# Adding up the seven products of a Strassen-like up projection in PSUM banks instead of on VectorE

## What is computed

```python
def rms_norm(x, g):
    xf = x.astype(jnp.float32)
    y = xf * lax.rsqrt(jnp.mean(xf * xf, axis=-1, keepdims=True) + EPS)
    return (y * g.astype(jnp.float32)).astype(x.dtype)

def sq_relu_mlp(h, w_up, w_down):
    return jnp.square(jax.nn.relu(h @ w_up)) @ w_down

# in each of the two layers
h = h + sq_relu_mlp(rms_norm(h, g_mlp[layer]), w_mlp_up[layer], w_mlp_down[layer])
```

## Time and profile before

| | us |
|---|---|
| median of 3 runs | 1628.29 |
| the runs | 1630.63, 1628.01, 1628.29 |
| the profiled execution | 1630.15 |
| its span | 1628.40 |

### The profile page before, as it was taken

One profiled execution on the slowest core, in us unless ns is written; L12 is line 12 of the kernel. 1 busy time (PEld: TensorE's weight loads), 2 busy tenths in 40 slices (PEclk: granted clock), 3 DMA queues, 4 the chain that ended last, 5 costly groups with the idle time before them and its releaser, 6 DMA issues.

```text
span 1628.4 us, 29172 instructions
## 1 busy us (share of the span) xinstructions
PE 1598.7 (98%) x12203; PEld 1417.2 (87%) x12203; DVE 1016.4 (62%) x1416; ACT 725.8 (45%) x1144; POOL 271.0 (17%) x222
## 2 busy tenths in 40 slices
PE   8999999999999999999999999999999999989998
PEld 7998677899999999999887898888887788667896
DVE  6534666388666666555557867677756547856544
ACT  5533554465444444331235544444445445675323
POOL 1002212132222222110004222222212000000200
PEclk9999999999999999999999999999999999999999
DMA  6231030123332222232232333222256676001001
GB/s 197 78 78 31 22 84 10 54 78 130 104 104 89 94 84 99 84 99 93 88 104 78 130 104 104 96 90 100 97 103 99 118 96 89 19 1 62 28 28 52
DMA packets 122689, 134.29 MB, mean 82 GB/s; under 512 B 18877, under 2 KB 99508, under 8 KB 122564
## 3 DMA queue, kind: packets, MB, share of 16 engines
q1 hardware_dynamic: 122362, 132.44, 29.7%
q10 hardware_dynamic: 202, 0.06, 0.0%
HBM read 126.13 MB, written 2.10 MB: 79 GB/s over the span
## 4 chain that ended last, share of the span: by engine, by line
PE 91%; DVE 4%; ACT 2%; issue 1%; DMA 1%; SPq 1%; ACTq 0%; DVEq 0%
PE ps L483 30%; PE ps L1703 22%; PE ps L1650 17%; PE ps L2699 2%; PE ps L829 2%; PE ps L1674 2%; PE ps L812 2%; PE ps L939 1%; PE ps L1220 1%; PE ps L2427 1%; PE ps L837 1%; PE ps L3224 1%; PE ps L2871 1%; PE ps L2850 1%; PE ps L2866 1%
## 5 line engine op out<-in xcount | busy, mean ns | idle before, releaser
L453 ACT ACTIVATE w_hi<-raw 128x1024 fp32r<-128x1024 f32 (+2 forms) x171 | 179.4, 1051 | 400.4 <-PE ps L483 249.4
L483 PE MATMUL ps<-x_hi,w_hi 128*128 128x512 f32 (+4 forms) x872 | 245.8, 333 | 0.5 <-DVE x_lo L503 0.4
L483 PE MATMUL ps<-x_lo,w_hi 128*128 128x512 f32 (+4 forms) x872 | 239.7, 326 | 0.0
L483 PE MATMUL ps<-x_hi,w_lo 128*128 128x512 f32 (+4 forms) x872 | 239.1, 325 | 0.0
L460 DVE TENSOR_TENSOR w_lo<-raw,w_hi 128x1024 fp32r<-128x1024 f32 (+2 forms) x171 | 206.5, 1222 | 45.1 <-ACT w_hi L453 45.1
L1703 PE MATMUL ps<-a_hi,w_hi 128*128 128x258 f32 (+1 forms) x768 | 204.2, 320 | 0.3 <-DVE h L1887 0.3
L1703 PE MATMUL ps<-a_hi,w_lo 128*128 128x258 f32 (+1 forms) x768 | 204.1, 320 | 0.0
L1703 PE MATMUL ps<-a_lo,w_hi 128*128 128x258 f32 (+1 forms) x768 | 204.0, 320 | 0.0
L483 PEld LDWEIGHTS ps<-x_hi,w_hi 128*128 128x128 f32 (+2 forms) x872 | 145.4, 187 | 19.2 <-issue 3.1
L483 PEld LDWEIGHTS ps<-x_lo,w_hi 128*128 128x128 f32 (+2 forms) x872 | 144.6, 186 | 16.4 <-issue 2.2
L483 PEld LDWEIGHTS ps<-x_hi,w_lo 128*128 128x128 f32 (+2 forms) x872 | 144.6, 187 | 14.7
(11 more groups left out here) (489 smaller groups left out, 3343.2 us busy)
## 6 DMA issues: line engine op xcount, KB each, us to landing
raw<-in_w_mlp_up SPq DMA_DIRECT2D x32, 1024.0 KB, 5.3
raw<-in_w_mlp_down SPq DMA_DIRECT2D x32, 1024.0 KB, 5.0
raw<-in_w_in SPq DMA_DIRECT2D x16, 1024.0 KB, 9.6
raw<-in_w_in_conv SPq DMA_DIRECT2D x12, 1024.0 KB, 5.0
raw<-in_w_in_attn SPq DMA_DIRECT2D x8, 1024.0 KB, 5.2
raw<-in_w_out_attn SPq DMA_DIRECT2D x4, 1024.0 KB, 5.0
raw<-in_w_out_conv SPq DMA_DIRECT2D x4, 1024.0 KB, 4.9
raw<-in_w_out SPq DMA_DIRECT2D x4, 1024.0 KB, 5.8
```

Of the source, the lines that this page charges most:

```text
L453: act.activation(split_tile(w_hi, t), raw_tile(t), ACT.Copy).then_inc(w_hi_ok, 1)
L483: ins = pe.matmul(tile_banks(t)[0:m, b, 0:c], w[:, k, :], x[:, k, x0:x0 + c], start=(k == order[0] and n == 0), stop=(k == order[-1] and n ...
```

## The change

The products run in the order 1, 7, 6, 2, 5, 4, 3. Bank 0 takes products 1, 6, 5 and 3 in turn, each accumulated on what is there. After product 1 ScalarE copies bank 0 into bank 1, in PSUM, and product 2 accumulates on that copy; the other two copies (bank 2 after product 7, bank 0 after product 6) go to SBUF as before. So the quarters "11" (bank 1) and "12" (bank 0) are finished in PSUM, and VectorE takes each out with one instruction that also does the maximum with zero and the scale. "22" and "21" stay one addition each, with one full-width scaling behind them. The sum "75" and the scaling of tile 0 are gone, bank 3 is no longer used by the products. TensorE waits for ScalarE's first copy ahead of product 6 (now third), for its third copy ahead of product 5 (now fifth) and for VectorE's "22" ahead of product 3 (now last). Tile 1 is squared and split before tile 0.

```diff
-        ORDER = (1, 5, 7, 2, 6, 3, 4)
+        ORDER = (1, 7, 6, 2, 5, 4, 3)
-        P_BANK = {1: 0, 6: 0, 2: 1, 7: 2, 4: 2, 5: 3, 3: 3}
+        P_BANK = {1: 0, 6: 0, 5: 0, 3: 0, 2: 1, 7: 2, 4: 2}
...
             if m == 1:
                 pe.wait_ge(w_lo_ok, t + 1)
-                if first:
-                    pe.wait_ge(evicted, MLP_T0[layer] + 2)
-                else:
-                    pe.wait_ge(copied, 3 * n)
-            if m == 5:
+                pe.wait_ge(evicted, MLP_T0[layer] + 2 if first else up_tile(layer, u - 1) + 2)
+            if m == 7:
                 pe.wait_ge(p_lo, 2 * n + 1)
                 if first:
                     pe.wait_ge(xs["lo"], 4 * layer + 4)
                 else:
-                    pe.wait_ge(added, 3 * n)
-            if m == 7 and not first:
-                pe.wait_ge(evicted, up_tile(layer, u - 1) + 2)
-            if m == 2 and not first:
-                pe.wait_ge(evicted, up_tile(layer, u - 1) + 1)
+                    pe.wait_ge(added, 2 * n)
             if m == 6:
                 pe.wait_ge(copied, 3 * n + 1)
                 pe.wait_ge(p_lo, 2 * n + 2)
-            if m == 3:
-                pe.wait_ge(added, 3 * n + 1)
+            if m == 5:
+                pe.wait_ge(copied, 3 * n + 3)
             if m == 4:
                 pe.wait_ge(w_lo_ok, t + 2)
                 pe.wait_ge(copied, 3 * n + 2)
+            if m == 3:
+                pe.wait_ge(added, 2 * n + 1)
...
-                    if m == 4 and k == 0 and j < 2:
+                    if m == 3 and k == 0 and j < 2:
                         ins.then_inc(mm_done, 1)
...
-            m, dst = ((1, s1), (7, s7), (6, s6))[which]
+            m, dst = ((1, ps[:, P_BANK[2], :]), (7, s7), (6, s6))[which]
             act.wait_ge(product, product_at(layer, u, m))
...
+            elif which == 0:
+                act.wait_ge(evicted, MLP_T0[layer] + 2)
             act.activation(dst[:, 0:hw], ps[:, P_BANK[m], 0:hw], ACT.Copy).then_inc(copied, 1)
...
             if what == "11":
                 dve.wait_ge(product, product_at(layer, u, 2))
-                dve.wait_ge(copied, 3 * n + 1)
-                dve.wait_ge(a_lo_ok, FF // P * layer + 2 * u - 1)
-                dve.tensor_tensor(tmp[:, 0, hw:2 * hw], s1[:, 0:hw], b1, ALU.add).then_inc(evicted, 1)
+                dve.wait_ge(a_lo_ok, read)
+                dve.scalar_tensor_tensor(tmp[:, 0, hw:2 * hw], b1, 0.0, scale_bc[:, f + hw:f + 2 * hw], ALU.max, ALU.mult).then_inc(evicted, 1)
...
+            if what == "22":
+                dve.wait_ge(copied, 3 * n + 2)
+                dve.wait_ge(product, product_at(layer, u, 5))
+                dve.tensor_tensor(tmp[:, 1, 0:hw], s7[:, 0:hw], b0, ALU.add).then_inc(added, 1)
...
             if what == "12":
                 dve.wait_ge(product, product_at(layer, u, 3))
-                dve.tensor_tensor(tmp[:, 0, 0:hw], s6[:, 0:hw], b3, ALU.add).then_inc(added, 1)
...
+                dve.scalar_tensor_tensor(tmp[:, 0, 0:hw], b0, 0.0, scale_bc[:, f:f + hw], ALU.max, ALU.mult).then_inc(evicted, 1)
...
-                add("75")
                 add("11")
                 add("22")
+                add("21")
+                scale_dve(dve, nm, layer, u)
                 add("12")
-                scale_dve(dve, nm, layer, u, 0)
-                add("21")
-                scale_dve(dve, nm, layer, u, 1)
...
             if u <= NU:
+                a_low(dve, nm, layer, u - 1, 1)
                 a_low(dve, nm, layer, u - 1, 0)
-                a_low(dve, nm, layer, u - 1, 1)
```

## The result

The changed kernel took 1640.52 us (median of 5 executions, 1636.55 to 1643.23), the kernel before 1629.76 us beside it (5 executions, 1628.01 to 1630.63). The ratio is 1.0069, with a 95% interval of 1.0051 to 1.0086. It is slower, as foretold, but by 10.8 us where 4.6 were forecast, and 1640.5 lies above the range of 1629.3 to 1636.6. The profiled execution took 1640.52 us, with a span of 1638.7; that of before had 1628.4. Between the two spans lie 10.3 us.

The account below looks back on a forecast made before the run. TensorE, busy 98% of the span, was taken as the bound. Two waits less one removed, 2.52 + 2.67 - 0.58 = +4.61 us on a median of 1628.29, gave 1632.9 us, range 1629.3 to 1636.6.

Parts of the forecast that it names:

- rival A: The clock falls in the two stalls of the layers' first up blocks, 1.7 us each: +8.0, 1636.3 us; chance 0.12.
- The waits: First up block of each layer: position 3 waits for ScalarE's late first copy, 2.52 us in layer 0, 2.67 in layer 1.
- The wait of L1698: Down block behind layer 1's first up block: its wait goes, -0.58 us, or about 0.1 won if low parts stay slow.
- The copy into PSUM: ScalarE's first copy taken as 0.39 us, bounds 0.21 and 0.78; shifts the two stalls by -0.36 to +0.78 us together.
- Settled blocks and VectorE's load: The 26 settled up blocks cost nothing, with 0.73 to 0.80 us of room; 36 us less on VectorE gains nothing.
- C: Less VectorE and ScalarE traffic speeds up the up blocks' matmuls; at 0.3 us per block -3.8, 1624.5 us; chance 0.04.
- D: Settled up blocks wait too; with a first copy of 1.3 us +9.8, 1638.1 us; chance 0.05.
- B: One of the two first-up-block stalls is not paid: +2.1 or +2.5, 1630.6 us, no net change; chance 0.17.
- the statement about later stages: Behind the changed blocks, a wait elsewhere follows TensorE's own work and moves along with the delay; no cost was added.

Follow-up runs that it names:

- e2: Changed kernel with 18 matmuls into free bank 3 ahead of the waiting product 6 in each layer's first up block; 1639.39 us, ratio 1.0059.
- e8: Changed kernel with ScalarE's first copy moved ahead of the weight splits in layer 0 only; 1634.56 us, ratio 1.0026.
- e3: Changed kernel with ScalarE's first copy moved ahead of the last plain square and both weight splits in each layer's first up block; 1628.61 us, ratio 0.9994.
- e9: Kernel before with 66 matmuls (7.9 us) added at the start of layer 0's first up block; 1637.31 us, ratio 1.0052.
- e4: Changed kernel with the first copy ahead of the splits and the second weight split behind the copies, in each layer's first up block; 1628.81 us, ratio 0.9996.
- e1: Kernel before with only a wait for ScalarE's first copy added at position 3 in each layer's first up block; 1636.45 us, ratio 1.0040.
- e5: Changed kernel, unaltered and measured anew; 1640.99 us, ratio 1.0067.
- e10: e4 with 66 matmuls added at the start of layer 0's first up block; 1639.02 us, ratio 1.0056.
- e11: e4 with 43 matmuls (5.1 us) added at the start of layer 0's first up block; 1636.59 us, ratio 1.0042.
- e12: Changed kernel with 8 matmuls (0.95 us) added in layer 1 at the start of the block behind the waiting one; 1637.65 us, ratio 1.0048.
- e15: Changed kernel with 28 matmuls (3.3 us) added in layer 1 at the start of the block behind the waiting one; 1643.55 us, ratio 1.0074.

## Why the prediction was right in part and wrong in size

The sum of the waits held. Two things were missing from it: the falls of the clock behind the waits, which the prediction had only as its rival A, and the late stretch, which it didn't have at all.

**The waits: right, place and size.** Layer 0: the waiting matmul would have started at 372.63 + 0.12 = 372.75 and started at 375.12, 2.37 late; the next start came 0.22 behind it where 0.12 is the rhythm, 0.10 of refill. That makes 2.47, and 2.52 was forecast. Layer 1: 911.33 less 2.44 of idle time and 0.28 of the last record puts that matmul's start at 908.61, so the natural start at 908.73; 2.60 and 0.10 make 2.70, forecast 2.67. As stages, without falls, the first measured 2.62 (e2) and the second 2.47 and 2.35 (e2, e8).

**The wait of L1698: right, and eaten up by small things.** In the down block behind the first up block of layer 1 the low parts ran free of GpSimd, as said, in 0.69 us each where before two of them took 3.52:

```profile
921.57 0.69 DVE L1820 TENSOR_TENSOR a_lo<-tmp,a_hi 128x512 fp32r<-128x512 f32 x1 [0.88 <-ACT a_hi L1735]
```

The wait is gone from the page. But of the 0.58 us only 0.2 to 0.35 stand in stage B (2.70 against 2.47 and 2.35), and e3, which has no such wait either, has a stage B of 650.77 against 650.72 of before. The price itself was right: in e9, the kernel before with nothing but a delay, the wait is gone as well and stage B is 650.15, 0.57 us shorter. In the new order it is used up in layer 1 by a first up block of 10.12 us against 9.96 (e3), by twelve settled up blocks that alternate between 9.97 and 9.94 us where before it was 9.95 and 9.94 (119.46 against 119.34 us in all), and by twelve down blocks of 11.14 us against 11.11 (133.68 against 133.35). Why these take longer was not looked into; the prediction had put them at nothing.

**The copy into PSUM: in its bounds.** Durations of the copies by destination (ns: least, median, most):

```profile
L1721 ACT ACTIVATE s<-ps x56: 364/387/389, 375.0 to 1188.8; 128x258 f32<-128x258 f32 x28, 128x256 f32<-128x256 f32 x28
L1721 ACT ACTIVATE ps<-ps x28: 362/368/370, 374.7 to 1186.0; 128x258 f32<-128x258 f32 x14, 128x256 f32<-128x256 f32 x14
```

0.37 us was measured where 0.39 was taken from the earlier trace rows. The Trainium skill (ScalarE: Activation LUTs, Step-by-step: what each stage is for), which says that ScalarE reaches PSUM faster, agrees with this trace, by 0.02 us.

**Settled blocks and VectorE's load: right.** The other 26 up blocks wait for nothing. A stretch of the chain in layer 0:

```profile
384.07 11.54 PE ps L1698 x96
...
438.88 10.05 PE ps L1645 x84
```

That is the 10.05 of the earlier trace rows; its down blocks take 11.54 to 11.61 us, around the 11.60 there. Rivals C (less traffic makes matmuls faster) and D (settled blocks wait) are refuted by these, C also by e3 and e4. B (a wait is swallowed) is refuted by the two waits of the changed kernel, which stages A and B both show at full price, and by e1.

**The clock: the first step that failed.** The prediction named the mechanism as rival A, priced it, and gave it 0.12, with the sentence that "the matmuls around these stalls are dense, those before the fall weren't". That reason was worth nothing: in 12 of 15 such waits the clock fell although the matmuls on both sides were dense. The price was right within 0.3 us: 1.53 and 1.44 measured by stages, 1.7 forecast. That waits and falls together came to 8.0 us in e5's stages, as rival A had said, is in part luck: its falls were 0.4 us too dear and its waits, less the 0.58, 0.5 us too cheap. The Trainium skill (TensorE: Matmul & The Clock Gate, Why this matters for your kernels) warns of idle gaps between bursts of matmuls only where they are longer than these. Here the clock fell at gaps of 2.2 to 2.5 us in 12 of 15 cases, so by the measurement shorter gaps count too. The step should have weighed as what they are, 1.3 us of idle time in 4 (4.00 - 2.73) followed by a fall, with waits of nearly twice that to come.

**The late stretch: what no step held.** The sum ended at the stages of the change, and the statement about later stages was that a delay moves along. The late part moves along, but it doesn't cost the same in every execution: 104.3 to 105.0 us undisturbed, 108.9 to 109.0 with 10.2 us at half clock, 110.0 to 110.2 with 13.7. A term of about 4.7 us for it was put at nothing. The kernel before has the late stretch seldom, if at all (none is profiled with it): its executions are mostly from 1627.8 to 1630.5, and four of the 23 beside e1 lie from 1632.3 to 1634.2. The changed kernel has it in nine of eleven, by the same measure.

**The sum as measured**, for the profiled executions: waits 2.62 + 2.47, falls 1.53 + 1.44, stage D 4.19 (late stretch 4.7, missing fall at 1508 us -0.5), the missing fall at 269 us -1.94, the untouched stages -0.01; together 10.3 us. The forecast had the first two terms, less 0.58, and nothing else. It also started from a median of before of 1628.29, which five executions put at 1629.76, so that against the forecast of 1632.9 the result is 7.6 us off and the difference 6.2.

**What stays open.** Why the late stretch comes in nine of eleven executions of the changed kernel and, by their times, in all of e2's, in one to three of six with a pure delay of 5 to 8 us, and in none of 22 of e3 and e4, isn't settled. That it needs the long waits or the falls behind them is excluded (e2 has no such fall, e10 neither, and both have it), and so is that they always bring it (e5 has both and is without it). Whether they make it more frequent isn't. That a shift of the late part alone can bring it is shown by e10 and e11 against e3 and e4 (5 of 12 executions by their times, two of them with a profile, against none of 22); that single microseconds decide is suggested by the steps of e12 to e15 within the spread of six executions. Which moment is a bad one can't be told from these traces, since executions of one kernel differ.

## What to carry to other kernels

When a change gives a wait less room, look at the first pass through the loop apart from the settled ones: there the releasing engine still comes from other work, and here all of the loss started from two places out of 28, while one instruction moved ahead of that work took all of it away. Count a wait of over 2 us on a TensorE that is otherwise busy as the wait plus a likely fall of its clock, unless rows of the same kernel show such a wait without one, and take the densest neighbourhood as no protection. A kernel whose later part runs small, dependent matmuls can answer a shift of a few us with several us of its own, and by e12 perhaps in either direction, so measure such a change over more executions and read the untouched stages too before explaining a difference by the edited one.

## What the runs showed of the hardware that I had not expected

- TensorE fell to half clock behind holes of 2.2 to 2.5 us amid dense matmuls in 12 of 15 profiled cases. By stages a fall cost 1.4 to 1.6 us. The same hole in e8 (2.42 us) had none behind it. When the hole was filled with matmuls (e2), both falls were absent.
- In stage D the clock was halved for 10.2 or 13.7 us while TensorE was busy for 3.7 to 4.0 of each 4 us, with short matmuls, in seven of sixteen profiled executions of the changed kernel and the experiments. It cost 4.7 us where it was 10.2 us long and 5.1 to 5.8 where it was 13.7, against executions that have or lack the fall near 1508 us as it does.
- Added work may make a program faster: with 0.95 us of matmuls more the median was 1637.65 (6 executions) against 1640.5 and 1641.0 (5 and 6). The intervals against before overlap, so this is a hint.
- A ScalarE copy of 256 to 258 fp32 columns took 368 ns into PSUM and 387 ns into SBUF (medians of 28 and 56).
